# Where the modulation chunks stand in a two-layer recurrent decoder trunk: bursts, a third group in three gaps, and two moved steps of the norm

## What is computed

```python
mods = (jax.nn.silu(c) @ ada_w + ada_b).reshape(B, 3, 3, 1, D_MODEL)
def modulate(t, i):
    return t * (1.0 + mods[:, i, 1]) + mods[:, i, 0]
def residual(t, i, out, w):
    return _layer_norm(ALPHA * t + w * (1.0 + mods[:, i, 2]) * out, ln_g[i], ln_b[i])
x = residual(x, 0, _swiglu(modulate(x, 0), ffn_wg[0], ffn_wu[0], ffn_wd[0]), 0.5)
proj = modulate(x, 1) @ w_in              # then the mixers
x = residual(x, 1, mix, 1.0)
x = residual(x, 2, _swiglu(modulate(x, 2), ffn_wg[1], ffn_wu[1], ffn_wd[1]), 0.5)
```

## Time and profile before

| | |
|---|---|
| runs | 1758.27 us median of 3 (1747.54, 1758.27, 1759.58) |
| profiled execution | 1754.12 us, its span 1752.0 us |
| busy | TensorE 95%, VectorE 54%, ScalarE 38%, GpSimd 9% |
| weights and the rest from HBM | 261.83 MB, 153 GB/s over the span |
| modulation chunks on TensorE | lines L1982 (matmuls) and L1992 (folds) |

### The profile page before, as it was taken

The page is one execution under the profiler, slowest core; times in us unless marked ns, Lnnn a source line. Parts: engine busy times, 40 slices in busy tenths (PEclk is TensorE's granted clock), DMA queues, the critical chain, the costliest instruction groups (busy, mean ns, idle before and its releaser), DMA issues.

```text
span 1752.0 us, 32980 instructions
## 1 busy us (share of the span) xinstructions
PE 1665.3 (95%) x14132; PEld 1522.3 (87%) x14132; DVE 951.6 (54%) x1631; ACT 664.6 (38%) x959; POOL 164.6 (9%) x219
## 2 busy tenths in 40 slices
PE   5999999999999999999999999999998999999997
PEld 2899998988678779999989999989877777899997
DVE  2444445584643676555464454466846446755544
ACT  2233334464223335433353333355622233543333
POOL 1000011100102131000110000110010123200011
PEclk9999999999985699999999999999999558999999
DMA  8655655433641064444635555644332204644441
GB/s 308 213 203 217 204 186 175 153 109 120 218 152 40 29 230 146 154 148 151 222 125 212 191 182 178 220 148 135 114 116 78 66 1 131 224 150 152 145 157 66
DMA packets 92512, 270.22 MB, mean 154 GB/s; under 512 B 27184, under 2 KB 29648, under 8 KB 92112
## 3 DMA queue, kind: packets, MB, share of 16 engines
q1 hardware_dynamic: 87952, 265.50, 44.5%
q10 hardware_dynamic: 4416, 2.62, 0.6%
HBM read 261.83 MB, written 6.26 MB: 153 GB/s over the span
## 4 chain that ended last, share of the span: by engine, by line
PE 79%; DVE 13%; DMA 3%; ACT 3%; issue 2%; SPq 0%; POOL 0%; ACTq 0%; DVEq 0%; POOLq 0%
PE psV L1967 12%; PE psV L1968 11%; PE psV L1969 11%; PE psA L1967 9%; PE psA L1969 8%; PE psA L1968 8%; DMA raw<-weights_dram 3%; PE psV L747 3%; DVE wlo L2280 2%; PE psY L1982 1%; PE psC L1982 1%; DVE PJ L1467 1%; ACT whi L2143 1%; DVE XL L2330 1%; PE psV L736 1%
## 5 line engine op out<-in xcount | busy, mean ns | idle before, releaser
L2280 DVE TENSOR_TENSOR wlo<-raw,whi 128x1024 fp32r<-128x1024 f32 x334 | 412.5, 1239 | 406.5 <-ACT whi L2143 403.8
L2143 ACT ACTIVATE whi<-raw 128x1024 fp32r<-128x1024 f32 x334 | 352.2, 1055 | 333.7 <-PE psV L1969 306.7
L1967 PE MATMUL psA<-XH,whi 128*128 128x320 f32 x1120 | 353.9, 316 | 11.4 <-DVE wlo L2280 10.5
L1968 PE MATMUL psA<-XL,whi 128*128 128x320 f32 x1120 | 348.6, 311 | 0.0
L1969 PE MATMUL psA<-XH,wlo 128*128 128x320 f32 x1120 | 348.5, 311 | 0.0
L1967 PE MATMUL psV<-XH,whi 128*128 128x320 f32 x848 | 268.9, 317 | 0.1
L1968 PE MATMUL psV<-XL,whi 128*128 128x320 f32 x848 | 264.7, 312 | 0.0
L1969 PE MATMUL psV<-XH,wlo 128*128 128x320 f32 x848 | 264.6, 312 | 0.0
L1967 PEld LDWEIGHTS psA<-XH,whi 128*128 128x128 f32 x1120 | 212.6, 190 | 25.4 <-issue 18.8
L1967 PE MATMUL psV<-HH,whi 128*128 128x320 f32 x704 | 217.5, 309 | 0.0
L1968 PE MATMUL psV<-HL,whi 128*128 128x320 f32 x704 | 217.5, 309 | 0.0
(11 more groups left out here) (398 smaller groups left out, 1933.4 us busy)
## 6 DMA issues: line engine op xcount, KB each, us to landing
raw<-weights_dram SPq DMA_DIRECT2D x450, 512.0 KB, 3.5
own<-weights_dram SPq DMA_DIRECT2D x20, 512.0 KB, 6.4
in_xh<-weights_dram SPq DMA_DIRECT2D x6, 512.0 KB, 4.6
raw<-weights_dram SPq DMA_DIRECT2D x8, 256.0 KB, 3.7
in_hl<-weights_dram SPq DMA_DIRECT2D x4, 512.0 KB, 6.1
ZS<-st_rw_dram SPq DMA_DIRECT2D x2, 768.0 KB, 5.3
S<-st_gla_dram ACTq DMA_DIRECT2D x2, 768.0 KB, 4.6
o_glas_dram<-S SPq DMA_DIRECT2D x2, 768.0 KB
```

Source lines behind the costliest of these rows:

```text
L1967: mm(out, split_hi(n)[:, k], hi[:, kt], start=first, stop=False)
L1968: mm(out, split_hi(n)[:, k], lo[:, kt], start=False, stop=False)
L2143: activation(split_hi(n), buffer(DENSE[n]), ACT.Copy).then_inc(hi_done, 1)
L2280: tt(split_lo(n), buffer(DENSE[n]), split_hi(n).bitcast(F32), ALU.subtract).then_inc(lo_done, 1)
```

## The change

The first up product takes its modulation chunks in bursts of four, followed by the previous group's fold (`ada_bursts`), each burst through the four buffers of `own`, whose loads stand in SP's stream six to nine dense chunks behind the previous burst. One group more stands in each of the three gaps behind a down product, (0,2,0), (1,1,0) and (1,2,0): the first and third come out of the two mixer tails, the second out of layer 1's up product. In these gaps one fold stands between the eighth and ninth chunk; eight of the twelve chunks have own buffers (two in XH's place, two in XL's, four in `own`), four use the ring. ScalarE copies the first group's rows ahead of the wait for the variance. VectorE's low half of the last locked chunk moves behind the variance's last step, as does the subtraction of the second ZT tile behind the first scaling; behind out, the low half of the third locked chunk also moves behind the last ZT tile. Silu's table is loaded behind the modulation.

```diff
@@ -160,9 +160,18 @@
     return out + [("fold", *groups[-1])]
-def two_groups(groups):
-    return [("ada", *group, q) for group in groups for q in range(4)], [("fold", *group) for group in groups]
+def ada_bursts(groups):
+    bursts = [[("ada", *group, q) for q in range(4)] + [("fold", *g) for g in groups[max(n - 1, 0):n]]
+              for n, group in enumerate(groups)]
+    return bursts + [[("fold", *groups[-1])]]
+def gap_groups(groups):
+    chunks, folds = [("ada", *group, q) for group in groups for q in range(4)], [("fold", *group) for group in groups]
+    return chunks[:8] + folds[:len(groups) - 2] + chunks[8:], folds[max(len(groups) - 2, 0):]
@@ -172,13 +181,14 @@
...
     def product(step, s, groups):
-        chunks, left = two_groups(groups)
+        chunks, left = gap_groups(groups)
         return [step, ("norm", L, s)] + chunks, left
...
-    out = after(spread([(step, int(k >= 2)) for k, step in enumerate(up[0])], ada_groups(in_ffn) if in_ffn else []), folds)
+    tiles = spread([([step], int(k >= 2)) for k, step in enumerate(up[0])], ada_bursts(in_ffn))
+    out = after([step for steps in tiles for step in steps], folds)
...
     out += steps
@@ -203,14 +213,15 @@
     out = ada_groups(groups(0, 0, 0, 1, 2, 3)) + [("enter", 0)]
     steps, left = layer_plan(0, groups(0, 0, 4, 5) + groups(0, 1, 0, 1, 2, 3),
-                             (groups(0, 1, 4, 5), groups(1, 0, 2, 3), groups(1, 0, 4, 5)),
-                             groups(0, 2, 0, 1, 2, 3, 4, 5) + groups(1, 0, 0, 1))
+                             (groups(0, 1, 4, 5) + groups(0, 2, 0), groups(1, 0, 2, 3), groups(1, 0, 4, 5) + groups(1, 1, 0)),
+                             groups(0, 2, 1, 2, 3, 4, 5) + groups(1, 0, 0, 1))
     out += steps
-    steps, left = layer_plan(1, groups(1, 1, 0, 1, 2, 3), (groups(1, 1, 4, 5), groups(1, 2, 4, 5), []), groups(1, 2, 0, 1, 2, 3), left)
+    steps, left = layer_plan(1, groups(1, 1, 1, 2, 3), (groups(1, 1, 4, 5) + groups(1, 2, 0), groups(1, 2, 4, 5), []),
+                             groups(1, 2, 1, 2, 3), left)
     return out + steps
-RAW, SPL, AHEAD = 4, 3, 6
+RAW, SPL, AHEAD = 4, 3, 8
 LOCK, LAST = 4, 2
@@ -234,16 +247,26 @@
             if kind == "ada" and left:
                 left -= 1
                 if n_end is None:
-                    steps.append((L, starts[item], False, True))
+                    steps.append((L, starts[item], False, 2 * AHEAD - 2 - left))
                 else:
-                    early.setdefault(n_end - 2 - left, []).append((L, starts[item], False, True))
+                    early.setdefault(n_end - 2 - left, []).append((L, starts[item], False, AHEAD - left))
                 continue
-            steps += [(L, starts[item] + c, kind != "ada", False) for c in range(CHUNKS_OF[kind])]
+            if kind == "gate" and of[1] == 0:
+                burst, in_up, later = sum(c[2] for c in steps), True, False
+            elif kind in ("down", "proj"):
+                in_up = False
+            if kind == "ada" and in_up:
+                early.setdefault(burst + (8 if later else 6) + of[2] // 2, []).append((L, starts[item], False, AHEAD - 3 + of[2]))
+                if of[2] == 3:
+                    later = True
+                    burst = sum(c[2] for c in steps)
+                continue
+            steps += [(L, starts[item] + c, kind != "ada", 0) for c in range(CHUNKS_OF[kind])]
             n_end = sum(c[2] for c in steps) if kind == "down" else None
@@ -268,13 +291,21 @@
...
 ADA = [m for m, c in enumerate(LOADS) if not c[2]]
-RING = [[m for m, c in enumerate(LOADS) if c[3] == own] for own in (False, True)]
+RING = [[m for m, c in enumerate(LOADS) if c[3] == own] for own in range(2 * AHEAD - 1)]
+OWN, PREVIOUS = [m for m, c in enumerate(LOADS) if c[3]], {}
+for _k, _m in enumerate(OWN):
+    _first = LOADS[_m][3] in (1, AHEAD + 1) or LOADS[_m][3] == AHEAD - 3 and LOADS[OWN[_k - 1]][3] != AHEAD - 4
+    PREVIOUS[_m] = (OWN[_k - 1] if _k else None) if _first else PREVIOUS[OWN[_k - 1]]
 GAPS = [n for n, step in enumerate(PLAN) if step[0] == "norm" and n + 1 < len(PLAN) and PLAN[n + 1][0] == "ada"]
 BEHIND_OUT = [k for k, n in enumerate(GAPS) if PLAN[n - 1][0] == "out"]
-IN_INPUT = {3 * PLAN[n][1] + PLAN[n][2]: sum(step[0] == "ada" for step in PLAN[:n]) + 2
+IN_INPUT = {3 * PLAN[n][1] + PLAN[n][2]: sum(step[0] == "ada" for step in PLAN[:n]) + 4
             for k, n in enumerate(GAPS) if k not in BEHIND_OUT}
+THREE = {3 * PLAN[n][1] + PLAN[n][2]: (PLAN[n + 1][1:4], sum(step[0] == "ada" for step in PLAN[:n]) + 4)
+         for n in GAPS if PLAN[n + 9][0] == "fold" and PLAN[n + 10][0] == "ada"}
@@ -462,10 +494,11 @@
...
-        own = ffn.take("own", [P, AHEAD - 2, 8, P])
+        own = ffn.take("own", [P, AHEAD - 4, 8, P])
         in_xh = nc.alloc_sbuf_tensor_at("in_xh", [P, 2, 8, P], F32, offset=xh_of_all)
+        in_xl = nc.alloc_sbuf_tensor_at("in_xl", [P, 2, 8, P], F32, offset=xl_of_all)
         in_hl = nc.alloc_sbuf_tensor_at("in_hl", [P, 2, 8, P], F32, offset=hl_end - 2 * 4 * 8 * P)
@@ -609,16 +642,20 @@
         def landed(m):
             ring = LOADS[m][3]
-            q, n = RING[ring].index(m), (RAW, AHEAD)[ring]
-            return (loaded, loaded_own)[ring][q % n], 16 * sum(1 + (LOADS[i][1] in HALVES) for i in RING[ring][q % n:q + 1:n])
+            q = RING[ring].index(m)
+            if ring:
+                return loaded_own[ring - 1], 16 * (q + 1)
+            return loaded[q % RAW], 16 * sum(1 + (LOADS[i][1] in HALVES) for i in RING[0][q % RAW:q + 1:RAW])
         def buffer(m):
-            q = RING[LOADS[m][3]].index(m)
-            if not LOADS[m][3]:
-                return raw[:, q % RAW]
-            if q % AHEAD > 1:
-                return own[:, q % AHEAD - 2]
-            return (in_hl if q // AHEAD in BEHIND_OUT else in_xh)[:, q % AHEAD]
+            place = LOADS[m][3] - 1
+            if place < 0:
+                return raw[:, RING[0].index(m) % RAW]
+            if place < 4:
+                return (in_xh, in_xl)[place // 2][:, place % 2]
+            if place < AHEAD:
+                return own[:, place - 4]
+            return in_hl[:, place - AHEAD] if place < AHEAD + 2 else own[:, place - AHEAD - 2]
@@ -1932,15 +1969,15 @@
...
-                    q, size = RING[ring].index(m), (RAW, AHEAD)[ring]
-                    if q >= size:
-                        last = RING[ring][q - size]
+                    q = RING[ring].index(m)
+                    last = PREVIOUS[m] if ring else RING[0][q - RAW] if q >= RAW else None
+                    if last is not None:
                         if LOADS[last][2]:
                             sp.wait_ge(lo_done, DENSE.index(last) + 1)
                         else:
                             sp.wait_ge(ada_used, ADA.index(last) + 1)
                     for L in range(DEPTH):
-                        if ring and m == min((e for e in RING[True] if e > DENSE[FIRST["out", L]]), default=None):
+                        if ring and m == min((e for e in OWN if e > DENSE[FIRST["out", L]]), default=None):
...
                             sp.wait_ge(*at("stored", 144))
@@ -1949,7 +1986,7 @@
                             sp.dma_start(buffer(m)[:, :, FH * h:FH * (h + 1)],
...
                     else:
-                        sp.dma_start(whole(buffer(m)), weights[l, n]).then_inc((loaded, loaded_own)[ring][q % size], 16)
+                        sp.dma_start(whole(buffer(m)), weights[l, n]).then_inc(loaded_own[ring - 1] if ring else loaded[q % RAW], 16)
@@ -2184,11 +2221,17 @@
                 def norm(s):
                     nc.scalar.preload_act_table_set("natural_log_exp_and_others")
+                    if s in THREE:
+                        rows(*THREE[s])
                     act.wait_ge(sem("var_ready"), s + 1)
                     rsqrt(A, VR[:], sem("sd_ready"))
+                    modulate(s + 1 if s < 3 * DEPTH - 1 else None, s)
                     if s % 3 != 0 and s < 3 * DEPTH - 1:
                         nc.scalar.preload_act_table(ACT.Silu)
-                    modulate(s + 1 if s < 3 * DEPTH - 1 else None, s)
+                def rows(group, used):
+                    act.wait_ge(ada_used, used)
+                    A.do(activation(MR[:, GROUPS.index(group) % 2], psM[BANK[group]][:, 0:256], ACT.Copy), sem("mrow_done"))
@@ -2206,9 +2249,8 @@
                         na += 1
                         if n_next and n_next not in OUTS:
                             split_to(n_next + (2 if n_next not in LOCKED else LOCK - 1))
-                        if of[2] == 3:
-                            act.wait_ge(ada_used, na)
-                            A.do(activation(MR[:, GROUPS.index(step[1:4]) % 2], psM[BANK[step[1:4]]][:, 0:256], ACT.Copy), sem("mrow_done"))
+                        if of[2] == 3 and (step[1:4], na) not in THREE.values():
+                            rows(step[1:4], na)
@@ -2330,7 +2372,7 @@
```

(19 more changed lines are left out.)

## The result

The kernel after took 1734.16 us, median of 4 runs (1729.39 to 1735.89); before, beside it, 1758.92 (1747.54 to 1761.54). The medians differ by 24.8 us. The ratio, taken over the runs side by side, is 0.9882, 95% interval 0.9852 to 0.9912: 20.8 us less (15.5 to 26.0). The profiled execution took 1735.18 us with a span of 1733.1, against 1754.12 and 1752.0: 18.9 less, where the prediction had 20.9.

The account below looks back on a forecast made before the run. TensorE's instruction stream was taken as the bound, busy 1665.3 of 1752.0 us. Terms of -9.0, -1.9, -3.6, -3.7, -0.4 and -2.3 summed to -20.9 us, giving 1733.2 to 1737.4; forecast 1736, range 1726 to 1752.

Parts of the forecast that it names:

- Terms 1 to 3: First up products: nine bursts -9.0 us, the stall for a chunk -1.9, a group leaving layer 1's up product -3.6.
- R1: Rival, up products: the clock falls behind the bursts, up to 28.8 us lost, 1765 and slower; chance 0.04.
- Term 5: Three gaps behind down products: twelfth chunk 1.1 us late, clock high, 22.4 us each, -0.4 in sum.
- R2: Rival, gaps: low clock behind down (+4.8), slower landings (+3.9), transfers bound behind out (+1.5), 1746 us; chance 0.20.
- Term 4: Both mixer tails: one group leaving each saves 1.85 us a group, -3.7 in sum.
- R3: Rival: drained switches hide half the bursts' 9.0 us, or a tail fills with waits, losing 3.7; 1744; chance 0.14.
- Term 6: Gaps behind out products: moved table load and low halves give -1.4 us in the first, -0.9 in layer 1's; -2.3 together.

Follow-up runs that it names:

- e1: Kernel after with the up products' modulation chunks single again, through the shared ring of four: 1743.66 us, ratio 0.9946 to the kernel before.
- f1: Kernel before with the bursts and the buffers alone: 1742.38 us, ratio 0.9919 to the kernel before.
- e2: Kernel after with the bursts kept but loaded through the shared ring of four: 1803.04 us, ratio 1.0268 to the kernel before.
- e4: Kernel after with only the two groups of the mixer tails put back there: 1736.18 us, ratio 0.987 to the kernel before.
- f2: Kernel before with all the moved steps of the norm and the buffers alone: 1751.46 us, ratio 0.9984 to the kernel before.
- e3: Kernel after with the three groups put back, two into the tails, one into layer 1's up product: 1734.26 us, ratio 0.9878 to the kernel before.
- f3: Kernel before with the third groups in the gaps behind down and the buffers alone, first MR copy ahead of the root: 1745.53 us, ratio 0.9949.
- e5: Kernel after with Silu's table loaded ahead of the modulation again: 1731.88 us, ratio 0.9871 to the kernel before.
- e6: Kernel after with the low half behind down products ahead of MN again: 1735.35 us, ratio 0.9882 to the kernel before.

## Why the prediction was right, point by point

The forecast was 1736 and the time is 1734.16; faster by 1.2% (0.9 to 1.5), as the likeliest case had it. Sum and steps, however, agree unevenly.

*Terms 1 to 3, right.* Bursts, stall and the group out of layer 1's up product were to give 14.5 and gave 14.8. The pair spacing of the gap, 0.43, was the right price inside a burst; e1 and f1 show the terms taken out and put in alone. One step stood on cover, ten microseconds between issue and use; from 50 us on the loads into `own` took 4.6 to 7.3 us (predicted 3.2 to 4.5) and those into the ring 3.0 to 6.0, and no burst waited. The 8.3 of layer 0's product is one profile's: the eight kernels with the same order there gain 6.7 to 9.0. e2 shows what the cover is worth. R1 fell with it: the clock behind the bursts stayed at 1.00. In e2, where TensorE stood still between the same narrow chunks, it fell.

*Term 5, right, and by its own chain.* 22.4 us in each of the three gaps, the twelfth chunk late by 0.7 instead of 1.1, the tiles 8.2 behind instead of 8.3, clock high. R2's stretches behind A, C and D did not come. e4, with eight chunks and 1.90 us idle, has the low clock at A again, and so has f2; but e3 and f1, which idle as long there (1.84 in f1), keep it high and take 14.9. With twelve chunks in A it stayed high in all eight kernels that have them.

*Term 4, wrong: "7.4 / 4 = 1.85 a group, -3.7".* The tails gave nothing (+1.2 and -1.0). The step took the difference of two tails, which also differ in layer, as a price per group, and held everything else in place. TensorE did save 2.2 and 2.5 us of busy time. In layer 1 a group less was worth some 2 us on the mean of the kernels (72.9 to 70.8), near the 1.85. In layer 0 it cost some 2 us (80.2 to 82.3): with seven groups spread over the tail the third one is complete 7.5 us later, its MR copy holds ScalarE and the gate rows behind it, and TensorE waits 5.24 us for Yb instead of 2.38. This is R3's second half, "a tail fills with waits", and the wait was made by the order of the steps: the prediction has no row of ScalarE in the tail. That copying MR behind the gate rows would bring the group's worth back is not shown; no run tried it.

*Term 6, -2.3: -0.9 in this profile, on the mean of nine -1.7.* In the profile after E gave 1.3 (predicted 0.9); B lost 0.4 where 1.4 was predicted, 0.5 gained in the out product and 0.9 lost in the tiles at the low clock. The step "the tiles can start at 659.4 instead of 660.41" held: it says 1.0 sooner, six kernels with the same steps behind out show 1.2 to 1.4. The last chunk comes 52.2 to 53.3 us behind out's first matmul whether the halves stand ahead or behind (52.9 before), as the prediction took it; the kernel after has the latest, 53.3. R2's third part, "in B and E transfers bound", is right for the start of the tiles, but didn't take the gain. The other step, tiles that "win 0.4 more", failed in B: they take 14.6 to 14.7 in all kernels but the one where the clock falls. Out, B and E together changed by -2.9 to +0.1 in the nine kernels with the halves behind. So what one profile shows of this term depends on where the clock falls, and its -0.9 alone doesn't prove the term too large.

*What was not forecast.* 1.9 us in the recurrences and 1.5 in the input projections, which made good most of what terms 4 and 6 lost. No step of the change shortens them, and both vary as much among the other kernels (the second projection stretch takes 113.1 to 115.3 us). So the near hit of the sum, 18.9 against 20.9, owes 3.4 us to places that had no term: that part is luck.

## What to carry to other kernels

Small work between large matmuls cost 0.77 us a piece alone and 0.43 behind another piece: gathering four cut their price from 3.08 to 2.03 us, but only with buffers of their own, loaded a whole burst ahead; through the shared ring the same order was 2.7% slower than before. Filling an idle gap with work from elsewhere pays only what that elsewhere is bound by: out of a product that TensorE bounds it gave 2.5 to 3.8 us a group. Out of a tail full of dependencies it gave some 2 us in one layer and cost some 2 in the other, because the pieces that stayed moved too: where every engine walks a fixed list, look what stands behind each piece on each engine's list, not only at the piece that goes. A step moved off one chain may also hold a buffer that another chain waits for, as the low half did for the twelfth chunk. And one profile a kernel places a gain of 1 us no better than the clock repeats itself: compare the same stage over all kernels that share it.

## What was unexpected on the hardware

*The first recurrence takes between 89 and 97 us with the same instructions.* Three kernels, the same 1108 or 1109 matmuls: before, e3, f3. The last columns are granted clock, DMA share and GB/s.

```profile
510.90:605.90 95.00, 90.33 (x1109) 73.36 (x1108) 45.05 (x102) 26.13 (x38) 17.82 (x12) 0.56 0.12 37
```

```profile
502.90:592.10 89.20, 84.25 (x1108) 68.84 (x1109) 44.88 (x102) 26.02 (x38) 17.81 (x12) 0.61 0.13 40
```

```profile
512.10:602.90 90.80, 86.14 (x1108) 70.90 (x1108) 44.91 (x102) 26.14 (x39) 17.80 (x12) 0.59 0.14 40
```

The shorter the stage, the higher its mean clock: 0.56, 0.59, 0.61. The clock has two levels, so a mean of 0.56 to 0.61 is an eighth to a fifth of the stage at 2.4 GHz and the rest at 1.2 (an estimate from the means). Both recurrences together took 183.3 us in e5 and 192.4 in f1. What decides it stays open; one profiled execution a kernel can't part an effect of the edit (where the stage starts) from chance. The values don't lie anywhere, though: before and e4 have 95.03 and 95.04, and e1, e5 and f3 90.75, 90.74 and 90.86. It is as large as most terms of this study, so stages should be compared without it.

*The same idle time, another clock.* Behind A, eight chunks and 1.84 to 1.90 us idle were followed by a low stretch in three kernels (before, e4, f2) and by none in two (e3, f1); one costs 15.7 - 14.9 = 0.8 there. Behind B, with stops of 0.30, 0.64 and 0.65 us between the chunks, the clock fell in the kernel after and in none of the twelve others, though e1, e4 and e6 have nearly the same stops (e1: 0.33, 0.64, 0.63). In layer 0's tail the mean clock is 0.98 in the five kernels with eight groups, where the wait for Yb is 2.4 us, and 0.94 or 0.96 in the eight with seven, where it is 5.2.
